# Down-projection of each pair of hidden tiles: token tile by token tile, with both column halves in turn

## What is computed

```python
def conv_ffn(x, w_up, w_dw, b_dw, w_down):
    h = depthwise_conv(x @ w_up, w_dw, b_dw)
    g, u = jnp.split(h, 2, axis=-1)
    return (jax.nn.silu(g) * u) @ w_down
...
        x = layer_norm(DEEPNORM_ALPHA * x + mix, ln_mix_g[i], ln_mix_b[i])
        f = conv_ffn(x, ffn_w_up[i], ffn_w_dw[i], ffn_b_dw[i], ffn_w_down[i])
        x = layer_norm(DEEPNORM_ALPHA * x + f, ln_ffn_g[i], ln_ffn_b[i])
```

## Time and profile before

| | |
|---|---|
| median of 3 runs | 3276.29 us |
| lowest and highest | 3274.36 and 3276.58 us |
| span of the profiled execution | 3272.1 us |
| TensorE busy in it | 3018.3 us (92%) |
| VectorE busy | 2044.5 us (62%) |
| GpSimd busy | 1034.4 us (32%) |
| ScalarE busy | 663.9 us (20%) |
| mean granted TensorE clock | 0.938 of full |

### The profile page before, as it was taken

One profiled execution on the slowest core, in us unless ns is written; L12 is line 12 of the kernel. 1 busy time (PEld: TensorE's weight loads), 2 busy tenths in 40 slices (PEclk: granted clock), 3 DMA queues, 4 the chain that ended last, 5 costly groups with the idle time before them and its releaser, 6 DMA issues.

```text
span 3272.1 us, 39469 instructions
## 1 busy us (share of the span) xinstructions
PE 3018.3 (92%) x14110; PEld 2408.7 (74%) x14110; DVE 2044.5 (62%) x2932; ACT 663.9 (20%) x1599; POOL 1034.4 (32%) x817
## 2 busy tenths in 40 slices
PE   8999859869999999999899899998699999999998
PEld 6888647757878878787578544577588887887874
DVE  2699854786665556555630499658766666556557
ACT  2222251401111101010231366403001111100102
POOL 3355202443323223322113233225432323322322
PEclk9999979989999999999699899999899999999996
DMA  3000003101111111111111000211011111111111
GB/s 121 26 26 26 13 1 110 39 20 39 33 39 35 32 35 38 35 32 32 45 59 49 17 4 1 81 39 39 26 36 36 37 34 38 32 32 39 39 30 64
DMA packets 156587, 123.58 MB, mean 38 GB/s; under 512 B 27889, under 2 KB 133785, under 8 KB 156472
## 3 DMA queue, kind: packets, MB, share of 16 engines
q1 hardware_dynamic: 149416, 96.33, 10.3%
q10 hardware_dynamic: 7056, 25.69, 2.1%
HBM read 111.51 MB, written 10.49 MB: 37 GB/s over the span
## 4 chain that ended last, share of the span: by engine, by line
PE 39%; DVE 9%; ACT 2%; issue 1%; POOL 0%; POOLq 0%; DVEq 0%; ACTq 0%
PE bank L592 11%; PE bank L595 11%; PE bank L597 11%; PE bank L912 3%; PE bank L888 2%; DVE up_conv L1365 1%; DVE gate_conv L1365 1%; PE bank L903 1%; DVE h_lo L1382 1%; DVE up_conv L1378 1%; ACT probs L1127 1%; DVE gate_conv L1361 1%; DVE y L1194 1%; DVE up_conv L1361 1%; DVE y L1196 0%
## 5 line engine op out<-in xcount | busy, mean ns | idle before, releaser
L592 PE MATMUL bank<-x_hi,w_hi 128*128 128x512 f32 (+1 forms) x2688 | 959.6, 357 | 56.6 <-ACT gate_up_raw L1066 27.2
L508 POOL CAST w_hi<-raw_pieces 128x512 fp32r<-128x512 f32 x348 | 374.1, 1075 | 1950.6 <-PE bank L592 1700.3
L595 PE MATMUL bank<-x_lo,w_hi 128*128 128x512 f32 (+1 forms) x2688 | 956.2, 356 | 0.0
L597 PE MATMUL bank<-x_hi,w_lo 128*128 128x512 f32 (+1 forms) x2688 | 955.7, 356 | 0.0
L592 PEld LDWEIGHTS bank<-x_hi,w_hi 128*128 128x128 f32 x2688 | 512.2, 191 | 131.4 <-ACT gate_up_raw L1066 28.1
L597 PEld LDWEIGHTS bank<-x_hi,w_lo 128*128 128x128 f32 x2688 | 511.9, 190 | 71.4
L595 PEld LDWEIGHTS bank<-x_lo,w_hi 128*128 128x128 f32 x2688 | 512.4, 191 | 70.6
L512 POOL TENSOR_TENSOR w_lo<-raw_pieces,w_hi 128x512 fp32r<-128x512 f32 x348 | 495.9, 1425 | 27.9
L592 PE MATMUL bank<-w_hi,h_hi 128*128 128x512 f32 x880 | 397.8, 452 | 90.0 <-DVE h_lo L1382 60.9
L1397 DVE TENSOR_TENSOR y<-y,bank 128x512 f32<-128x512 f32 x440 | 295.6, 686 | 244.6 <-PE bank L597 242.2
L595 PE MATMUL bank<-w_lo,h_hi 128*128 128x512 f32 x880 | 379.6, 431 | 0.0
(11 more groups left out here) (131 smaller groups left out, 3235.3 us busy)
## 6 DMA issues: line engine op xcount, KB each, us to landing
raw_pieces<-in_ffn_w_up_dram SPq DMA_DIRECT2D x168, 256.0 KB, 2.9
raw_pieces<-in_ffn_w_down_dram SPq DMA_DIRECT2D x84, 256.0 KB, 2.6
raw_pieces<-in_conv_w_pw_dram SPq DMA_DIRECT2D x48, 256.0 KB, 2.7
y<-in_x_prompt_dram ACTq DMA_DIRECT2D x16, 512.0 KB, 8.4
residual_dram<-y ACTq DMA_DIRECT2D x10, 512.0 KB, 2.7
y<-residual_dram ACTq DMA_DIRECT2D x10, 512.0 KB, 9.5
out_dram<-y SPq DMA_DIRECT2D x10, 512.0 KB, 2.6
raw_pieces<-in_attn_w_q_dram SPq DMA_DIRECT2D x32, 128.0 KB, 2.4
```

The lines of the kernel that those rows point to most:

```text
L508: pool.tensor_copy(WH[:, p % RING, :], raw[:, p % RAW, :]).then_inc(piece_hi, 1)
L592: mm = pe.matmul(out, left[0], right[0], start=first, stop=False)
L595: pe.matmul(out, left[0], right[1], start=False, stop=False)
L597: return pe.matmul(out, left[1], right[0], start=False, stop=last)
```

## The change

In each of the 10 groups of a layer the 20 bank-fulls are taken in another order: `m` is now `2 t + n`. For each token tile the left and the right half follow each other. TensorE waits once, at the group's first bank-full, for all four pieces of `w_down`, where it waited for two and later for the other two. VectorE's adds follow the same order; those between convolution and `split_hidden` are now the two halves of token tile 0. In a layer's first group the residual waits move with them.

```diff
@@ TensorE, two_groups
                         for f in range(2):
                             up_tile(p + 4 * f, i, 6 * g + 3 * f, first)
-                        for n in range(2):
-                            pe.wait_ge(piece_split, i * 24 + p + 8 + 2 * n + 2)
-                            for t in range(TT):
-                                down_bank(p + 8, i, 20 * g + TT * n + t, t, n, 6 * g + 3, (P, P), first)
+                        pe.wait_ge(piece_split, i * 24 + p + 12)
+                        for t in range(TT):
+                            for n in range(2):
+                                down_bank(p + 8, i, 20 * g + 2 * t + n, t, n, 6 * g + 3, (P, P), first)
@@ VectorE, two_groups
                         def first_adds():
 
-                            for t in range(2):
-                                add_down(i, 20 * g + t, t, 0)
+                            for n in range(2):
+                                add_down(i, 20 * g + n, 0, n)
...
                                 if first and g == 0 and 3 * f + ch == 5:
-                                    dve.wait_ge(*RES_DONE(use - 1, 1))
+                                    dve.wait_ge(*RES_DONE(use - 1, 0))
...
-                        for n in range(2):
-                            for t in range(2 if n == 0 else 0, TT):
-                                if first and g == 0 and n == 0:
-                                    dve.wait_ge(*RES_DONE(use - 1, t))
-                                add_down(i, 20 * g + TT * n + t, t, n)
+                        for t in range(1, TT):
+                            if first and g == 0:
+                                dve.wait_ge(*RES_DONE(use - 1, t))
+                            for n in range(2):
+                                add_down(i, 20 * g + 2 * t + n, t, n)
```

## The result

| | before | changed |
|---|---|---|
| median | 3275.32 us (4 runs, 3274.17 to 3276.58) | 3291.06 us (4 runs, 3286.43 to 3293.88) |
| ratio, 95% interval | | 1.0047 (1.0032 to 1.0061) |
| the same once more | 3274.55 us (10 runs) | 3291.63 us (5 runs), 1.0054 (1.0041 to 1.0068) |
| span of the profiled execution | 3272.1 us | 3284.6 us (its own time 3286.43 us) |
| mean granted clock in it | 0.938 | 0.939 |

The change makes the kernel slower by 0.5%. The forecast was 3292 us.

What follows compares the result with a forecast made beforehand. TensorE, busy 3018 of 3272 us, was taken as the bound, through its idle time and half-clock time. Terms 0 + 15.0 + 0.3 = +15.3 us on 3276.3 gave 3291.6, say 3292 us; range 3275 to 3307.

Steps and rivals of the forecast that it cites:

- (a): Down-projection head: the wait for chunk 1 of `h` goes, the fifth bank-full still waits for VectorE's add until 10.2 us; gain 0.
- (b): 18 steady groups: half clock after the fifth bank-full's start loses 1.80 us per group against 0.97 before; +15.0 us.
- three rows of before: Times from TensorE's resumption to the clock's rise, 3.47, 4.31 and 4.14 us, whose mean 3.97 us set the loss per group.
- the costly form: Kernel before: groups with 4.31 us at half clock behind the fifth bank-full's start, losing 1.96 us, said to alternate with free ones.
- The fourth row: First layer's first group: clock back 5.89 us after resumption, after 4.27 us idle; left out of the mean, used for the range.
- (c): First group of each layer: no change in the first layer, +0.3 us in the second; residual waits 0.
- (d): Down-projection head: one wait for all four weight pieces, already split; later splits and loads lie beside idle time; cost 0.
- (e): Later bank-fulls: adds shorter than six matmuls, chunk 2 of `h` wanted later, no weight load saved; cost 0.
- Heavier: Rival: 5.89 us at half clock after each resumption in the groups, +31 us, 3307 us; chance 0.10.
- no difference: Rival: same clock loss as before, 0.97 us per group, 3276 us; chance 0.14.
- faster: Rival: clock granted again by the time TensorE resumes, no group pays, -17.5 us, 3259 us; chance 0.06.
- The layer's end: Rival: in the last down-projection the clock might stay up, -12 us, with the +15 about 3280 us; chance 0.07.

Runs made afterwards that it cites:

- kernels with early adds: Changed kernel with VectorE's first two, or first four, adds ahead of the convolution of the group's last chunk: 3263.09 us and 3222.28 us.
- two kernels with filler: Extra matmuls, result unused, in TensorE's down-projection stalls: 20 per group in the changed kernel, 3250.6 us; 10 and 7 in the kernel before, 3252.04 us.
- best against best: Changed kernel with VectorE's adds spread among the chunks' splits and convolutions, 3163.63 us, against the kernel before with four adds ahead of the last chunk's convolution, 3225.5 us.
- adds in the same places: VectorE's adds spread alike among the chunks' splits and convolutions: on the changed kernel 3163.63 us, on the kernel before 3293.55 us.
- the best kernel without useless work: Changed kernel with VectorE's adds spread, one token tile at a time, around chunk 1's split and the last chunk's convolutions: 3163.63 us, ratio 0.9662.
- the same order with four early adds: Kernel before, with VectorE's first four adds moved ahead of the convolution of the group's last chunk: 3225.5 us, ratio 0.9848.
- the new order with four early adds: Changed kernel with VectorE's first four adds moved ahead of the convolution of the group's last chunk: 3222.28 us, ratio 0.9838.

## Why the prediction was right, point by point

**The wait for chunk 1 (a).** Right. It went and gained nothing; the fifth bank-full starts after 10.22 us, predicted 10.2. That VectorE's add sets it is shown by the kernels with early adds, where it starts after 7.5 us.

**The clock (b).** Right in mechanism, a little small in size: +0.83 us per group, +15.0 in all, was predicted; the steady groups took 7.4 + 9.9 = 17.3 us more in the first profile and 16.4 in the second. The term that was small is the time at half clock behind the resumption: I took 3.97 us from three rows of before; over the 18 groups it is 4.4 us in the first profile and 4.3 us in the second, and where the pattern has settled 3.3, 4.3 and 6.2 us in turn. Two of my three rows did not measure what the term needs: 3.47 and 4.14 us run from a resumption to the rise, but only 3.41 us of each are at half clock. With these the mean is 3.7 us and the forecast +13. The loss before was 18.8 us and not 17.5, since the costly form comes first and last in each layer, 10 times in 18. The fourth row, 5.89 us, which I set aside as coming once, stood for something that now comes in each third group. My sentence that no row shows the clock rise while TensorE stands still was wrong: in the ninth group it rises at 1421.45, in the idle 0.64 us ahead of 1421.53. It does so in 9 places of the trace of before, always within 0.6 us of work; in the changed kernel the rise comes behind the resumption in all 18 groups, so the sum stands. The two kernels with filler show that the clock is all there is between the orders. What sets which of the three lengths a group gets stays open; a group's length depends on when it starts, and its own loss shifts the next start, but no run here pins that down.

**First groups (c).** Right: 0 and +0.4 us (predicted 0 and +0.3).

**Weight pieces (d) and the rest (e).** Right. The one wait costs 0 (1.0001). The splits moved to the end of the down-projection; GpSimd waits 27 us there, and the last of its four ends at 1460.50, 6 us ahead of VectorE's next chunk:

```profile
1452.74 0.61 POOL L508 CAST w_hi<-raw_pieces 128x512 fp32r<-128x512 f32 x1 [27.07 <-PE bank L592]
```
```profile
1466.66 0.55 DVE L1361 TENSOR_SCALAR gate_conv<-gate_up_raw,ffn_conv_table 128x511 f32<-128x511 f32 x1 [11.50 <-ACT gate_up_raw L1066]
```

**The rivals.** Heavier, no difference and faster did not come. The layer's end did shift in one of two profiles of the changed kernel (-7.5 us), on top of the forecast and not in place of it. I had given it 0.07, arguing that the clock fell after such a wait in every group; it does still fall, but it came back 14 us earlier. This and the 2.4 us at the start can be most of what the measured 3286 to 3294 us spread over; only two of the nine runs have a profile, so it is not shown. By luck the median hit the forecast within 1 us while the term (b) was 2 us small: the kernel before measured 3275.3 and later 3274.5 us, not the 3276.3 I started from, and some runs of the changed kernel came out short.

**The rule of the page.** The Trainium skill (TensorE: Matmul & The Clock Gate, HAM oscillation) prices throttled time at one half of it. Both kernels have 95.6 us of it in their steady groups in the first profiles, which is 47.8 us by that rule, an estimate, and yet they differ by 17 us; at 0.454 the kernel before loses about 19 us, the changed one about 36. Here the measurement decides: throttled time cost 0.454 us per us where it lay behind the start of the fifth bank-full, and nothing ahead of it.

## What to carry to other kernels

Before a wait is taken away, look at what the next instruction behind it waits for: if that comes later anyway, the gain is zero, and the stall, now in one piece, can cost clock. Time at half clock cost only where it lay over work on the path, so ask not how long the clock is low but what runs under it. An order change and the consumer's program belong together: the same order that lost 0.5% alone was worth 1.9% (best against best) to 3.9% (adds in the same places) once VectorE's adds came as the bank-fulls did, and the best kernel without useless work ran 3.4% below the start (3163.6 us).

## What the hardware showed that I had not expected

The same 2.3 us stall of TensorE was followed by half clock in 18 of 18 groups of the kernel before, and in 8 of 18 of the same order with four early adds. Stalls of 1.7 and 0.8 us in the new order with four early adds left the clock at full in 18 of 18.

In the last pair of the first layer, whose second product has 64 rows in place of 128, the clock stayed at half through 68 us in which TensorE was busy for 61 us, the first 39 us of them without a break; in the changed kernel's other down-projections it was back 3.0 to 6.2 us after work resumed. Kept at full by filler, it stayed there for the first 27 to 29 us of the same products. That the 64 rows are the reason is not shown; no run changes them.
